# Transposed keys of a paged-attention decoder step: two buffers of two pages for two of four

## The reference

```
k_past = cache_k[l][page_table].reshape(bs, n_pages * PAGE_SIZE, AT_HEADS, AT_DH)
v_past = cache_v[l][page_table].reshape(bs, n_pages * PAGE_SIZE, AT_HEADS, AT_DH)
...
gate = jnp.einsum('bhqd,bnhd->bhqn', qh, kmean)
gate = jnp.where(past_ok[None, None], gate, -jnp.inf)
_, sel = lax.top_k(gate, ksel)
...
s_sel = jnp.einsum('bhqd,bhqkld->bhqkl', qh, k_sel)
...
p = jax.nn.softmax(jnp.concatenate([s_sel, s_own], axis=-1), axis=-1)
```

## Time and profile before

| what | value |
|---|---|
| time, 3 runs | 767.29, 769.31, 772.36 us, median 769.31 |
| profiled execution, first to last instruction | 767.2 us (no time of its own beside the span is given) |
| TensorE matmul, weight load busy | 654.4 us, 549.4 us |
| VectorE, ScalarE, GpSimd busy | 409.3 us, 267.9 us, 86.0 us |
| transposes of keys, first to last start | 216.0 to 326.1 us |
| mean granted clock of TensorE | 0.903 of 2.4 GHz |

### The profile page before, as it was taken

One profiled execution on the slowest core, in us unless ns is written; L12 is line 12 of the kernel. 1 busy time (PEld: TensorE's weight loads), 2 busy tenths in 40 slices (PEclk: granted clock), 3 DMA queues, 4 the chain that ended last, 5 costly groups with the idle time before them and its releaser, 6 DMA issues.

```text
span 767.2 us, 13224 instructions
## 1 busy us (share of the span) xinstructions
PE 654.4 (85%) x5195; PEld 549.4 (72%) x5195; DVE 409.3 (53%) x496; ACT 267.9 (35%) x382; POOL 86.0 (11%) x110
## 2 busy tenths in 40 slices
PE   4769999999945767758989689973999999999995
PEld 1268999899933656534524259962999999999993
DVE  0552322425579979964368435649435353543526
ACT  1244323533472212121121333433546464532412
POOL 2050000000053265001111100002100000000000
PEclk9979999999985998965597979996999999999997
DMA  8876887685457978987597998631165546445301
GB/s 329 310 287 220 296 309 272 247 304 193 152 195 226 307 278 292 343 274 255 194 345 266 381 339 275 207 111 55 58 185 153 174 145 187 150 152 182 96 1 62
DMA packets 94257, 168.93 MB, mean 220 GB/s; under 512 B 6449, under 2 KB 37865, under 8 KB 91010
## 3 DMA queue, kind: packets, MB, share of 16 engines
q1 hardware_dynamic: 76562, 137.68, 52.3%
q10 hardware_dynamic: 14368, 19.86, 7.8%
q0 software_dynamic: 3280, 10.71, 3.6%
HBM read 163.51 MB, written 4.72 MB: 219 GB/s over the span
## 4 chain that ended last, share of the span: by engine, by line
PE 70%; DVE 14%; DMA 4%; ACT 4%; issue 3%; POOL 2%; ACTq 1%; SPq 0%; DVEq 0%
PE ps L1248 18%; PE ps L1250 17%; PE ps L1249 17%; DVE KT L939 3%; PE ps L1396 3%; PE ps L1259 3%; PE ps L1458 2%; DMA ring<-w_in 2%; DMA ring<-cache_v 1%; PE ps L1427 1%; DMA ring<-w_ada 1%; DVE hx L1096 1%; PE ps L1377 1%; PE ps L1303 1%; PE ps L1590 1%
## 5 line engine op out<-in xcount | busy, mean ns | idle before, releaser
L814 DVE TENSOR_TENSOR w_lo<-ring,w_hi 128x1024 fp32r<-128x1024 f32 (+1 forms) x128 | 152.2, 1216 | 148.4 <-ACT w_hi L479 148.3
L1248 PE MATMUL ps<-h_hi,w_hi 128*128 128x288 f32 x704 | 211.8, 301 | 19.1 <-POOL h_lo L386 19.1
L1249 PE MATMUL ps<-h_lo,w_hi 128*128 128x288 f32 x704 | 209.3, 297 | 0.0
L1250 PE MATMUL ps<-h_hi,w_lo 128*128 128x288 f32 x704 | 208.5, 296 | 0.0
L479 ACT ACTIVATE w_hi<-ring 128x1024 fp32r<-128x1024 f32 (+1 forms) x128 | 129.9, 1043 | 164.1 <-PE ps L1250 92.9
L1248 PEld LDWEIGHTS ps<-h_hi,w_hi 128*128 128x128 f32 x704 | 133.6, 190 | 26.8 <-issue 13.4
L1250 PEld LDWEIGHTS ps<-h_hi,w_lo 128*128 128x128 f32 x704 | 134.1, 190 | 0.0
L1249 PEld LDWEIGHTS ps<-h_lo,w_hi 128*128 128x128 f32 x704 | 133.8, 190 | 0.1
L939 DVE STREAM_TRANSPOSE KT<-ring 128x2048 f32<-128x2048 f32 x32 | 72.0, 2280 | 1.8 <-PE ps L1377 1.8
L1377 PE MATMUL ps<-KT,Wk 128*32 128x128 f32 x1024 | 41.0, 315 | 31.7 <-DVE KT L939 31.7
L1377 PEld LDWEIGHTS ps<-KT,Wk 128*32 128x32 f32 x1024 | 32.1, 126 | 40.4 <-DVE KT L939 27.1
(11 more groups left out here) (285 smaller groups left out, 850.7 us busy)
## 6 DMA issues: line engine op xcount, KB each, us to landing
ring<-w_ada SPq DMA_DIRECT2D x24, 1024.0 KB, 6.9
ring<-cache_k SPq DMA_DIRECT2D x96, 256.0 KB, 4.0
ring<-w_in SPq DMA_DIRECT2D x22, 1024.0 KB, 10.2
ring<-w_gu SPq DMA_DIRECT2D x44, 512.0 KB, 4.7
ring<-cache_v SPq DMA_DIRECT2D x64, 256.0 KB, 6.4
ring<-w_down SPq DMA_DIRECT2D x10, 1024.0 KB, 5.0
ring<-cache_k ACTq DMA_DIRECT2D x32, 256.0 KB, 3.8
ring<-cache_v ACTq DMA_DIRECT2D x32, 256.0 KB, 5.5
```

The lines of the kernel that those rows point to most:

```text
L814: dve.tensor_tensor(w_lo[:, par, k, :], slot4(s)[:, k, :], w_hi[:, par, k, :].bitcast(F32), ALU.subtract).then_inc(sem("lo_split"), 1)
L1248: pe.matmul(dst, h, x_hi, start=first, stop=False)
L1249: pe.matmul(dst, h, x_lo, start=False, stop=False)
L1250: return pe.matmul(dst, l, x_hi, start=False, stop=last)
```

## The change

KT keeps two buffers, of two pages each for four. A unit is turned in two halves, each of two of its pages (1024 columns), half h into buffer h. TensorE scores a half with 16 matmuls of 64 columns, so 32 for a unit where there were 16, into 64 of the unit's 128 columns of PSUM. `kt_turned` takes the place of `key_slots` and counts halves, and so does `kt_used`. Half h of a unit may be turned when half h of the unit before has been scored; before, a unit could be turned when the unit two places before had been scored. The waits of SP, ScalarE and GpSimd for a free slot are rewritten to the new counts and name the same point, the end of the whole unit's turning.

```diff
-    KT = sb("KT", [P, 2, 4, 512], F32, "split_area")
+    KT = sb("KT", [P, 2, 2, 512], F32, "split_area")
...
-                    sp.wait_ge(sem("key_slots"), b * 4 + (j - 3))
+                    sp.wait_ge(sem("kt_turned"), b * 8 + (2 * j - 6))
...
-            sp.wait_ge(sem("kt_used"), 4 * NSEQ)
+            sp.wait_ge(sem("kt_used"), 8 * NSEQ)
...
-                        act.wait_ge(sem("key_slots"), 4 * b + j - 3)
+                        act.wait_ge(sem("kt_turned"), 8 * b + 2 * j - 6)
...
-                act.wait_ge(sem("kt_used"), 4 * (b + 1))
+                act.wait_ge(sem("kt_used"), 8 * (b + 1))
...
-                if u >= 2:
-                    dve.wait_ge(sem("kt_used"), u - 1)
-                dve.transpose(KT[:, u % 2, :, :], ring[:, KV_SLOT[u % 4], :].rearrange("p (g n) -> p g n", n=512)).then_inc(sem("key_slots"), 1)
+                for half in range(2):
+                    if u:
+                        dve.wait_ge(sem("kt_used"), 2 * u + half - 1)
+                    dve.transpose(KT[:, half, :, :], ring[:, KV_SLOT[u % 4], half * 1024:(half + 1) * 1024].rearrange("p (g n) -> p g n", n=512)).then_inc(sem("kt_turned"), 1)
...
-                pe.wait_ge(sem("key_slots"), u + 1)
-                for m in range(4):
-                    for a in range(PAIRS):
-                        c = 4 * a + m
-                        ins = pe.matmul(ps[32 * a:32 * a + 32, b % 2, j * P:(j + 1) * P], Wk[:, b, m // 2, 2 * a + m % 2, :], KT[:, u % 2, :, c * 32:(c + 1) * 32],
-                                        start=m == 0, stop=m == 3)
-                ins.then_inc(sem("kt_used"), 1)
+                for half in range(2):
+                    pe.wait_ge(sem("kt_turned"), 2 * u + half + 1)
+                    for m in range(4):
+                        for a in range(PAIRS):
+                            c = 4 * a + m
+                            ins = pe.matmul(ps[32 * a:32 * a + 32, b % 2, j * P + half * 64:j * P + half * 64 + 64], Wk[:, b, m // 2, 2 * a + m % 2, :],
+                                            KT[:, half, :, c * 32:(c + 1) * 32], start=m == 0, stop=m == 3)
+                    ins.then_inc(sem("kt_used"), 1)
```

More of the change, by code:

```diff
@@ L312, in _ @@
                 pages = page_numbers(SPE, j, 2, NPG)
-                sp.wait_ge(sem("key_slots"), 4 * NSEQ - 3 + j)
+                sp.wait_ge(sem("kt_turned"), 8 * NSEQ - 6 + 2 * j)
                 load_pages(sp, "cache_v", pages, j, 0, "v_landed")
-            sp.wait_ge(sem("kt_used"), 4 * NSEQ)
+            sp.wait_ge(sem("kt_used"), 8 * NSEQ)
             for g in range(4):
@@ L442, in _ @@
                 pages = page_numbers(POOLE, 3 * NPG + j, 1)
-                pool.wait_ge(sem("key_slots"), 4 * NSEQ - 3 + j)
+                pool.wait_ge(sem("kt_turned"), 8 * NSEQ - 6 + 2 * j)
                 load_pages(pool, "cache_v", pages, j, 3, "v3_landed")
@@ L629, in value_pages @@
                     if b == 0:
-                        act.wait_ge(sem("key_slots"), 4 * NSEQ - 3 + j)
+                        act.wait_ge(sem("kt_turned"), 8 * NSEQ - 6 + 2 * j)
                     else:
```

## The result

The changed kernel is slower. In runs beside each other on one chip it took 780.68 us (median of 4, 778.86 to 783.52) against 768.30 us for the kernel before (4, 763.64 to 772.36), a ratio of 1.015 (1.011 to 1.020). A second series of the same changed kernel gave 1.011 (1.007 to 1.014). The time lies in the range, the direction is right, and the forecast of +7.2 us was too small: the two series give +11.8 (8.5 to 15.0) and +8.3 us (5.5 to 11.0).

The account below looks back on a forecast made before the run. VectorE was taken to bound the cached-key stage. With the clock as now 3.1 + 0.8 + 5.2 - 1.4 = 7.7 us, at full clock 5.9; 7.2 was taken, so 769.3 + 7.2 = 776.5 us, range 771.5 to 785.

Parts of the forecast that it names:

- the clock as it lies: Cached-key stage: half-clock stretches of TensorE stay where the trace had them; sum 7.7 us, against 5.9 us at full clock.
- Steps 1 to 3: From the 24 transposes to the sums of 289.54: shorter lead delays second gram +1.7, third +3.0, sums +3.0 to +3.2 us.
- the walk: Place-by-place count through the key stage of VectorE's waits for TensorE: whole kernel 773 to 780 us, chance 0.64.
- step 1: At the 24 transposes on TensorE: unit 8 waits to 251.5, ends at 253.8; first gram unmoved at 255.9 to 256.0.
- step 2: Unit 10's first half waits for unit 9's, scored behind the first gram, until 258.7; second gram to 261.6, +1.7 us.
- Step 4: After the sums of 289.54: transposes +0.8 us; stops behind restrip and gram or states +2.5 us, with half-clock stretches +5.2.
- Step 5: End of the key stage: last unit's scoring is only a half, -0.5 us at full clock, -1.4 with the trace's clock.
- the first part: Delay up to the sums of 289.54, entered in the total as 3.1 us.
- Dear halves: TensorE's scoring: a half costs as much as a whole unit; +10.6 to +19 us; chance 0.17, shared with a lower clock.
- Full clock: Key stage: smaller, more even pieces keep TensorE at full clock; +1.5 us, 771 us; chance 0.10.
- Faster: Key stage: first half scored while the second is turned, a head start; with full clock -4 us, 765 us; chance 0.04.
- Late pages: Key stage: pages arrive later than VectorE asks, so the halves don't show; 769 to 770 us; chance 0.05.

Follow-up runs that it names:

- the run that keeps the lead: The changed kernel with four half buffers of KT instead of two, so VectorE may again be two units ahead: 771.43 us, ratio 1.003 to the kernel before.
- scores first: The kernel before with ScalarE copying a sequence's scores into S ahead of the exponential that waits for GpSimd: 769.51 us, ratio 0.997.

## Why the prediction was right, and where it was too small

**The mechanism.** Right, as told: TensorE leaves the keys for other work, and a lead of one unit doesn't cover it. The predicted stops (8, 10, 14, 18, 22, 26, and with the clock as it lies 20 and 30) are eight of the ten measured. Unit 16 (1.12 us) was not foreseen; it stands behind the gram of 279.51, which took 3.78 us at half clock. Unit 29 has 0.23. "Some 10 us" of waits were 14.4. VectorE's two idle spells shrank to 0.75 and 0.60 us, not 1.3. The last block sum, told near 341, came at 344.96, of which 1.3 us is the later start.

**Steps 1 to 3.** Taking off the 1.3 us by which the stage starts later, the first gram is at 256.8 for 255.9, the second at 262.7 for 259.95, the third at 271.5 for 267.5, the fourth sums at 293.7 for 289.54: +0.9, +2.8, +4.0, +4.15, where the walk had 0, +1.7, +3.0 and +3.0 to +3.2. Every difference between the walk's steps is right within 0.3 us; what was wrong is "unmoved" for the first gram. The chain above says why. The 24 transposes start at the same place of the stage as before (248.58 - 217.32 = 31.3 us, 247.22 - 216.00 = 31.2), so nothing ahead of them makes the difference. But step 1 let unit 8 be turned at once when they end, at 251.5, and left out that the first half of unit 7 must be scored and given back first: 0.63 + 0.09 = 0.7 us, which step 2 did count. Measured, with the 1.3 us taken off, unit 8 is turned from 252.2 on, 0.7 later. And the copy of the raw scores, which was to be independent of this, stands on ScalarE behind a load that waits for unit 8.

**Step 4.** Predicted +0.8 and +5.2 us with the clock as it lies. The stops behind the fourth sums are 0.49 + 2.12 + 1.05 + 0.23 + 0.99 = 4.9 us, with the gap of 0.27 us between halves 5.2. The sum is right, but by luck: its parts were off in opposite directions. The stops at full clock, in front of units 22 and 26, cost 2.12 + 1.05 = 3.2 us for 2.5: behind unit 20 ScalarE still had an exponential and two loads ahead of its copy, so restrip began 1.6 us after the turning and not 1.05, and the gram had its small part of 0.34 us behind it. What hangs on half clock was 0.49 + 0.23 + 0.99 + 0.27 = 2.0 us for 2.7.

**Step 5.** The credit of 1.4 us was 0.7: the wait in front of the last sums went from 5.25 to 4.59 us. The last half took 1.08 us, and restrip and the copies behind it cost what they did. The 1.4 doesn't follow from the prediction's own prices either: from 1.75 us to a half at half clock, about 1.2, is 0.55.

The term that was mis-sized is thus the first part (1.0 us, the missing half of unit 7 most of it), then the end (0.7), and 0.5 us between the fourth and the last sums that I can't place; the value taken, 7.2, was another 0.5 under the walk's own 7.7. Together these are the 2.7 us between 7.2 and 9.9. They decide the side of the 1% line as well: I had 0.50 on within 1% and 0.46 on slower, with 7.2 us just under the bound of 7.7, and what was measured lies above it.

**The prices.** A half's transpose: 1135 ns in a row, as forecast (two and two are 4.62 us, less 1.21, over three is 1.137). A half's scoring: 0.65 us for 0.63. The Trainium skill's floor of about 25 ns between the starts of matmuls ("TensorE: Matmul & The Clock Gate", section "Wait — 56ns, not 53.3ns?") would have made the half 0.8 us if it counted each record. Counted so, the trace disagrees: 32 records, the last of 0.22 us, in 0.65 us are (0.65 - 0.22) / 31 = 14 ns apart. Counted by matmul, two records each, they are 28 ns apart, which a floor of 25 ns would allow.

**The rivals.** Dear halves: refuted by the run with only the scoring cut (their lower price adds up to 5.9 + 5.0 = 10.9 us, not 10.6). Full clock: the clock was 0.80 and 0.85, close to the 0.81 and 0.83 before. Faster: the head start itself is there. When unit 6 has been turned, TensorE begins the 24 transposes 1.1 us later, where it took 2.0 before, both at half clock, and that made up for VectorE's later arrival. It doesn't make the kernel faster: the run that keeps the lead is 0.3% (0.0 to 0.6) slower. Late pages: no wait for a page of keys after the change.

## What to carry to other kernels

How far one engine may run ahead must cover the longest stretch in which its consumer does other work, not the time for one piece: here a piece was handed back in 0.8 us and a lead of 2.3 us still cost 7 us, since behind unit 20, where restrip and a gram stand, the next half was back only 5.6 us after the turning (302.6 to 308.2). Before paying for a second buffer, look at the order in which the consumer leaves: here moving a 1 us step one place later gave 8.2 of the 9.9 us back with half the memory. And move the user of a step along with it; restrip alone made the kernel with lead slower, restrip and sums together made it 0.5% faster than before, and so faster than both kernels.

## What I had not expected of the hardware

One subtraction of the recurrence on VectorE, 128x1024, took 1.18 us before and 2.06 us after, with nothing in it changed. Before, the timelines of VectorE and then of GpSimd:

```profile
231.24 1.18 DVE L992 TENSOR_TENSOR hkt<-hb 128x1024 f32<-128x1024 f32 x1
```

```profile
231.20 2.15 POOL L415 TENSOR_TENSOR hx<-hb 128x512 f32<-128x512 f32 x1
233.31 1.08 POOL L416 TENSOR_TENSOR hx<-hb 128x512 f32<-128x512 f32 x1
```

After, the same two:

```profile
232.50 2.06 DVE L993 TENSOR_TENSOR hkt<-hb 128x1024 f32<-128x1024 f32 x1
```

```profile
232.41 1.07 POOL L415 TENSOR_TENSOR hx<-hb 128x512 f32<-128x512 f32 x1
233.44 2.02 POOL L416 TENSOR_TENSOR hx<-hb 128x512 f32<-128x512 f32 x1
```

Two instructions meet: in each kernel one of them has its normal 1.1 to 1.2 us and the other engine's, issued beside or behind it, is about 1 us too long. Before, VectorE's was short and GpSimd's took 2.15 us; after, GpSimd's was 1.07, VectorE's took 2.06, and GpSimd's next one 2.02. They don't run side by side, one waits the other out. VectorE's next subtraction, 128x128, took 1.16 and 1.12 us for an eighth of the columns; it meets GpSimd's in the same way. The Trainium skill says this of such pairs ("SBUF — State Buffer", section "Who interferes with whom"): VectorE and GpSimd share a pair of ports as a lock, and a VectorE instruction with two inputs in SBUF contends with a GpSimd instruction that reads SBUF; the trace agrees. Which of them waits turned on very little: VectorE's started 0.03 to 0.05 us behind GpSimd's in the six kernels with whole transposes, three of them short (before, the scoring cut, scores first) and three long. With half transposes it started 0.09 to 0.10 us behind and was long in all eight profiles. So this 0.9 us is no part of the lead, but it isn't the halves' own either, since three kernels with whole transposes had it too.

A matmul of 64 columns on four groups of output partitions takes about half of what one of 128 columns takes: at full clock 64 records in 1.10 us, so 14 ns a record and 56 ns a bunch of four, for 64 records in 1.95 us.
